# Lag products of a state-space recurrence placed right behind the state products, with their matrices finished earlier on VectorE

## The reference, cut to what matters

```
for direction in range(2):
    lam_bar = exp(lam * dt)
    b_bar = ((lam_bar - 1) / lam)[:, :, None] * b_mat
    bu = einsum('blgh,gph->blgp', uf, b_bar)
    _, state = associative_scan(op, (lam_bar, bu), reverse=(direction == 1))
    y = y + real(einsum('blgp,ghp->blgh', state, c_mat))
y = gelu(y); y = y * sigmoid(y @ w_glu + b_glu)
```

## Time and profile before

| | |
|---|---|
| median of three runs | 2506.31 us |
| profiled execution, its own time | 2506.62 us |
| its span, first to last instruction | 2505.1 us |
| TensorE busy | 2435.8 us, 97% |
| VectorE, ScalarE, GpSimd busy | 1798.5, 1204.0, 249.4 us |
| mean granted clock of TensorE | 0.991 of full |

### The profile page before, as it was taken

How to read it: one execution, slowest core, us unless ns; L and a number is a source line. 1 busy time by engine, 2 the same in 40 slices (tenths; PEclk the granted TensorE clock), 3 DMA queues, 4 the chain that set the end, 5 groups by cost and what they waited for, 6 DMA issues and landing times. The chain is left out here.

```text
span 2505.1 us, 44867 instructions
## 1 busy us (share of the span) xinstructions
PE 2435.8 (97%) x15016; PEld 2000.4 (80%) x15016; DVE 1798.5 (72%) x3171; ACT 1204.0 (48%) x2166; POOL 249.4 (10%) x478
## 2 busy tenths in 40 slices
PE   6999999999999999999989999999999999999998
PEld 5888888877777778898778888888777777788986
DVE  7888888627777876566678888885477777755666
ACT  5455555534443434453455555555344444444535
POOL 3421212100000000000043121211000000000000
PEclk9999999999999999999999999999999999999998
DMA  7555555444453435555565555554444534365554
GB/s 255 183 177 172 179 173 176 139 153 152 151 173 122 136 117 189 187 176 171 166 209 174 172 178 176 176 175 142 150 146 143 185 110 152 116 194 192 169 176 143
DMA packets 124620, 414.92 MB, mean 166 GB/s; under 512 B 19812, under 2 KB 26010, under 8 KB 124240
## 3 DMA queue, kind: packets, MB, share of 16 engines
q1 hardware_dynamic: 107424, 391.17, 47.3%
q0 software_dynamic: 17072, 22.18, 3.0%
HBM read 406.06 MB, written 7.21 MB: 165 GB/s over the span
## 5 line engine op out<-in xcount | busy, mean ns | idle before, releaser
L393 ACT ACTIVATE WH<-ring 128x512 fp32r<-128x512 f32 x1364 | 854.7, 632 | 1105.7 <-PE bank L1641 468.9
L407 DVE TENSOR_TENSOR WL<-ring,WH 128x512 fp32r<-128x512 f32 x852 | 573.2, 689 | 406.5 <-ACT WH L393 403.5
L1683 PE MATMUL bank<-XX,WH 128*128 128x512 f32 x2304 | 826.8, 402 | 34.3 <-DVE XX L596 15.7
L1685 PE MATMUL bank<-XX,WL 128*128 128x256 f32 x2304 | 647.7, 281 | 0.0
L1683 PEld LDWEIGHTS bank<-XX,WH 128*128 128x128 f32 x2304 | 436.5, 189 | 142.8 <-issue 21.0
L1641 PE MATMUL bank<-WH,XX 128*128 128x512 f32 x1536 | 485.4, 397 | 4.8 <-issue 3.5
L398 DVE TENSOR_TENSOR WL<-ring,WH 128x512 fp32r<-128x512 f32 x512 | 350.1, 688 | 128.0 <-ACT WH L393 125.5
L1685 PEld LDWEIGHTS bank<-XX,WL 128*128 128x128 f32 x2304 | 438.7, 190 | 0.0
L1641 PEld LDWEIGHTS bank<-WH,XX 128*128 128x128 f32 x1536 | 285.0, 188 | 81.5 <-issue 22.3
L1641 PE MATMUL bank<-WL,XX 128*128 128x512 f32 x768 | 299.6, 390 | 0.0
L1641 PEld LDWEIGHTS bank<-WL,XX 128*128 128x128 f32 x768 | 144.2, 188 | 31.1
(11 more groups left out here) (316 smaller groups left out, 3079.1 us busy)
## 6 DMA issues: line engine op xcount, KB each, us to landing
ring<-in_blocks SPq DMA_DIRECT2D x738, 512.0 KB, 3.3
ARENA<-in_bc POOLq DMA_DIRECT2D x2, 2048.0 KB, 8.9
ARENA<-in_decay POOLq DMA_DIRECT2D x8, 512.0 KB, 4.4
ARENA<-in_x SPq DMA_DIRECT2D x4, 512.0 KB, 9.1
u_scratch<-ARENA POOLq DMA_DIRECT2D x16, 128.0 KB, 3.4
ARENA<-u_scratch POOLq DMA_DIRECT2D x128, 16.0 KB, 3.0
ARENA<-lag_scratch POOLq DMA_DIRECT2D x128, 16.0 KB, 2.7
y_scratch<-ARENA POOLq DMA_DIRECT2D x16, 128.0 KB, 4.3
```

The lines of the kernel that those rows point to most:

```text
L393: nc.scalar.activation(wh[q], raw(which[0], q), ACT.Copy).then_inc(wh_ready[q], 1)
L407: vec.tensor_tensor(wl[q], raw(which[0], q), wh[q].bitcast(F32), ALU.subtract).then_inc(w_used[slot(which[0], half)], 1)
L1683: ins = mm(bank[b][:, :], h, xx[:, :, k, :], start=(k == 0), stop=(k == DT - 1), skip_group_check=True)
L1685: ins = mm(bank[b][:, 0:T], l, xh[:, k, :], start=False, stop=(k == DT - 1), skip_group_check=True)
```

## The change

On TensorE `lags()` moves from behind block 3 to right behind `inputs()`, ahead of block 3. Its waits stay at its beginning. On ScalarE the copy to LAG moves from behind the eviction of block 3 to behind that of block 2. On VectorE the second half of F (two products and their combination) moves ahead of two WL quarters of block 3, `wl_for(2, 2)` and `wl_for(2, 3)`, and the first product also ahead of `wl_for(2, 1)`. The subtraction L784 signals `f_ready` in place of VectorE's own step counter, so `f_ready` now rises twice in a turn, and the waits count by two.

```diff
-DVE_STEPS, DVE_S5_STEPS = 421, 21
+DVE_STEPS, DVE_S5_STEPS = 413, 20
...
                     st.wait()
-                    st.did(v.tensor_tensor(F[:, 0:40 * 16], ft[0], ft[1], ALU.subtract))
+                    v.tensor_tensor(F[:, 0:40 * 16], ft[0], ft[1], ALU.subtract).then_inc(f_ready, 1)
                     wl_for(2, 0)
-                    st.wait()
+                    dve.wait_ge(f_ready, layer * (2 * WT) + (ct * 2 + 1))
+                    st.did(v.tensor_tensor(terms(T1, 5), cr, g_i, ALU.mult))
                     wl_for(2, 1)
-                    st.did(v.tensor_tensor(terms(T1, 5), cr, g_i, ALU.mult))
-                    wl_for(2, 2)
+                    st.did(v.tensor_tensor(terms(T2, 5), ci, g_r, ALU.mult))
                     add_block(1)
-                    st.did(v.tensor_tensor(terms(T2, 5), ci, g_r, ALU.mult))
-                    wl_for(2, 3)
                     st.wait()
                     v.scalar_tensor_tensor(out=F[:, 40 * 16:80 * 16], in0=ft[0], scalar=-1.0, in1=ft[1],
                                            op0=ALU.mult, op1=ALU.subtract).then_inc(f_ready, 1)
+                    wl_for(2, 2)
+                    wl_for(2, 3)
                     wl_for(3, 0)
...
                     evict(2)
+                    full(4, "s5", ct * 2 + 1)
+                    free(a.activation(LAG, bank[4][:, 0:LAGS * 16], ACT.Copy), 4)
                     split_high(3)
                     evict(3)
-                    full(4, "s5", ct * 2 + 1)
-                    free(a.activation(LAG, bank[4][:, 0:LAGS * 16], ACT.Copy), 4)
...
-                        pe.wait_ge(f_ready, layer * WT + (ct + 1))
+                        pe.wait_ge(f_ready, layer * (2 * WT) + (ct * 2 + 2))
...
                     inputs()
+                    lags()
                     block_at(3)
-                    lags()
                     block_at(4)
```

More of the change, by code:

```diff
@@ L804, in _ @@
                     dve.wait_ge(phase_ready, layer * WT + (ct + 1))
-                    dve.wait_ge(f_ready, layer * WT + (ct + 1))
+                    dve.wait_ge(f_ready, layer * (2 * WT) + (ct * 2 + 2))
                     of_class = lambda b, s_: b.rearrange("p (m s c) -> p s m c", s=2, c=HOPS)[:, s_].unsqueeze(1).to_broadcast([P, 2, 4, HOPS])
```

## The result

The changed kernel took 2529.15 us (median of 2526.42, 2529.15 and 2531.73), the kernel before 2506.31. The ratio is 1.009, with a 95% interval from 1.0067 to 1.0113. The forecast was 2513.3 us with a range up to 2520, so the sign was right and the size was not: 22.8 us instead of 7. The profiled execution took 2526.42 us.

A forecast was written before the change was run, and what follows sets the result against it. TensorE, busy 97%, was taken as the bound: block 3 starts 1.30 us later, 0.86 comes back, so 0.44 a turn, 7.0 us over sixteen turns; 2506.62 + 7.0 = 2513.6 profiled, 2513.3 us median, range 2507.5 to 2520.

The forecast's parts named there:

- F complete 1.4 us after the inputs begin: On VectorE in the fourth turn: F ends at 243.86 us, 1.43 us earlier than in the kernel before.
- The sum of six rows: VectorE's chain from block 3's first WL quarter at 240.05 us through products, add and combination, ending at 243.86.
- The wake-up: Delay from F's completion on VectorE to TensorE's first lag matmul: between 0.14 and 0.48 us, taken as 0.30.
- The group itself: Lag products on TensorE at their new place ahead of block 3: 0.68 us from their start to the next wide matmul.
- 0.86 comes back behind it: On TensorE between blocks 3 and 4: removing the lag products there saves 0.86 us a turn.
- The 0.77 us of the old place: On TensorE between blocks 3 and 4: the gap shrinks from 0.88 to 0.11 us without the lag products.
- the 0.09 of the slow pair: First wide pair behind a small group on TensorE takes 0.33 instead of 0.24 us; one fewer gives back 0.09.
- The price of a wide pair: Each pair of wide matmuls on TensorE was counted at 0.35 us.
- F in time would be worth 3.5 us: Rival: VectorE finishes F before TensorE needs it, so merged small groups save 3.5 us, 2502.8 us in all; chance 0.06.
- The clock: Rival: TensorE's clock falls to 1.2 GHz in every turn, 1.5 us each, 2537 us in all; chance 0.07.
- The refill: Rival: TensorE's sequencer feeds 40 lag matmuls slowly into an empty queue, 2.3 us instead of 0.5, 2542 us; chance 0.03.
- Costed at nothing: Side effects priced at zero: WL quarters behind F, ring half blocks, ScalarE's LAG copy, VectorE's new wait, GpSimd's lag matrices.

The follow-up runs named there:

- add_early: Changed kernel with add_block(2), which frees bank 0, moved ahead of block 4's four WL quarters: 2516.18 us, 1.0042 of the kernel before.
- f_early: Changed kernel with F's second half made ahead of all WL quarters of block 3, add_block(2) left in place: 2517.03 us, 1.0043 of the kernel before.
- both_early: Changed kernel with F's second half ahead of all block 3 WL quarters and add_block(2) ahead of block 4's: 2507.97 us, 1.0004 of the kernel before.
- lags_only: Kernel before with only the change's TensorE and ScalarE moves, VectorE's order as before: 2568.33 us, 1.0242 of the kernel before.
- dve_only: Kernel before with only VectorE's part of the change, lag products and LAG copy still behind block 3: 2507.46 us, 1.0006 of the kernel before.
- nudge: both_early plus two already met waits between the lag products and block 3: 2508.64 us, 1.0001 of the kernel before.
- nudge4: both_early plus four already met waits between the lag products and block 3: 2507.51 us, 1.0006 of the kernel before.
- nudge8: both_early plus seven already met waits between the lag products and block 3: 2510.85 us, 1.0017 of the kernel before.

## Why the prediction was wrong

**F complete 1.4 us after the inputs begin: right.** The sum of six rows gave 243.86 - 242.45 = 1.41 us, the trace 249.44 - 248.00 = 1.44. The wake-up, bounded by 0.14 and 0.48, was 0.31. That the value taken was 0.30 is luck: no row chose it between the bounds. The group itself cost 250.38 - 249.75 = 0.63 us instead of 0.68, and with that block 3 starts 1.29 us later, against 1.30.

**"0.86 comes back behind it": this is the step that failed.** The 0.77 us of the old place and the 0.09 of the slow pair were read as the price of the lag products there. They were also the time in which VectorE freed bank 0. With them gone 0.74 and 0.09 are paid again, as a wait for L725: 0.83 us a turn, 13.3 us in all, and add_early takes back 13. The prediction listed what it costed at nothing and what hides it, but asked this only of what the change moves. `add_block(2)` moves nowhere in the changed part; it lost its cover, and the list did not have it. It could have been seen: in the trace before, L725 ends at 249.83, 0.65 us behind the start of block 3's last L1685, and block 4 starts at 250.06. Had it been in the sum, the forecast would have been 2513.3 + 13.3 = 2526.6 us, with 2529.15 measured.

**The price of a wide pair: mis-sized.** 0.35 us was used everywhere. Blocks 4 to 6 of the kernel before ran at 0.3467 in every turn, and in the changed kernel lose this in 11 of 16. Over all blocks it is (90 - 54) x 0.107 = 3.8 us, 0.24 a turn. The sum is now 1.29 - 0.86 + 0.83 + 0.24 = 1.50 us a turn, and the trace has 1.49.

**F in time would be worth 3.5 us: wrong for the same two reasons.** f_early has F in time and is 11 us slower than before for the bank; both_early has neither wait and is level for the rhythm.

**The clock: held, and the runs bear out the reason given.** The idle time of 0.6 to 0.7 us was not enough; 2.0 us in lags_only was, in 14 of 16 turns.

**The refill: refuted.** Behind the wait, with nothing queued, the 40 lag matmuls took 0.63 us from the first of them to block 3, 16 ns each, no more than the 0.68 of the earlier trace rows. The Trainium skill ("TensorE: Matmul & The Clock Gate", "Wait — 56ns, not 53.3ns?") gives about 62 ns per matmul where hardware decoding is off; for the group that is an estimate of 2.5 us by the 40 of the trace, and of 1.2 us by the 20 of the program. The trace has half of the smaller one, so it speaks against this case and agrees with the other, decoding in hardware without that price.

**Costed at nothing, and right:** the two WL quarters behind F and the moved copy on ScalarE. No wait of TensorE in the changed kernel has L398 as its releaser, dve_only is level, and both_early, which holds both moves, shows no third wait.

## What to carry to other kernels

A small group between two wide blocks has two values: what it costs, and what it hides. Before counting its price as a gain, look at what ends shortly before the next block starts, on every engine that releases a bank or a buffer for it; if it ends within the group, the gap remains when the group is gone, and if a wait is to be moved away the releaser's order must be changed with it. Where an engine is 97% busy, measure the repeated unit separately in each place: 2% in a pair of matmuls was as much as the whole gain that was sought.

## What the runs showed of the hardware

- Identical wide pairs, 512 and 256 columns at full clock and without idle time, ran at 0.3467 or 0.3533 us a pair for whole stretches of up to four blocks. Which of the two is settled when the stretch begins.
- TensorE started 0.31 us after VectorE's L792 had ended, with two further waits already met to be handled.
- The granted clock fell to 0.50 for over 3 us behind waits of 2.0 us in 14 of 16 turns (lags_only), and behind none of the waits of 0.6 to 0.7 us. Behind a wait of 3.0 us it was lower in one profile (before, from 479 us) and 1.00 in another (after, from 490 us), so the length of the wait does not decide it alone.
- Waits already met, between the lag products and block 3: two did not delay the block in 15 of 16 turns (nudge), four delayed it by about 0.25 us (nudge4), seven by 0.57 (nudge8).
